# Moving first loads of a stage into the stage before it, and shortening the router's choose and place steps, in a two-layer GLA / RG-LRU / mixture-of-experts kernel

## The reference, cut to what matters

```python
for layer in range(DEPTH):                       # 2
    if layer % 2 == 0: x = x + gla_mixer(x, ...)
    else:              x = x + rglru_mixer(x, ...)   # y @ w_out inside
    x = x + hier_moe(x, ...)
return rmsnorm(x, final_norm)

def hier_moe(x, norm_w, w_group, w_expert, w_gate, w_up, w_down):
    h = rmsnorm(x, norm_w)
    g_sel = argmax(h @ w_group)                  # one group of 4
    logits = (h @ w_expert)[group g_sel]         # its 8 experts
    top_p, top_e = top_k(softmax(logits), 2)
    weights = p_g * top_p / sum(top_p)
    eid = g_sel * 8 + top_e
    # tokens are sorted by expert in blocks of 128 rows, and for each block
    y = (silu(xb @ w_gate[e]) * (xb @ w_up[e])) @ w_down[e]
    # summed per token with its two weights
```

## Time and profile before

| | us |
|---|---|
| median of three runs | 3212.1 |
| profiled execution, its own time | 3209.87 |
| its span | 3208.1 |
| route0 from / experts0 from | 878.7 / 1156.2 |
| lru from / route1 from | 1714.6 / 2280.2 |
| experts1 from / finish from | 2557.7 / 3096.5 |
| TensorE matmul busy | 2677.0 (83%) |
| VectorE busy | 1824.7 (57%) |
| ScalarE busy | 1626.1 (51%) |
| POOL busy | 588.3 (18%) |

### The profile page before, as it was taken

The page is one execution under the profiler, slowest core; times in us unless marked ns, Lnnn a source line. Parts: engine busy times, 40 slices in busy tenths (PEclk is TensorE's granted clock), DMA queues, the critical chain, the costliest instruction groups (busy, mean ns, idle before and its releaser), DMA issues. The chain is left out here.

```text
span 3208.1 us, 43209 instructions
## 1 busy us (share of the span) xinstructions
PE 2677.0 (83%) x12246; PEld 2126.9 (66%) x12246; DVE 1824.7 (57%) x3426; ACT 1626.1 (51%) x2253; POOL 588.3 (18%) x795
## 2 busy tenths in 40 slices
PE   4999969999789949999993999999599588999940
PEld 3777756777678837777772777777488466777730
DVE  3444443434356656657653688886466667656645
ACT  3445444444334436556653666666344266555533
POOL 0000000000001134545450000000011144545420
PEclk9999979999989979999996999999799789999975
DMA  3111121111154359888876445422444299977857
GB/s 102 44 46 52 35 83 39 32 47 52 59 199 144 124 197 325 282 281 293 299 245 223 163 167 172 167 99 86 159 138 144 86 342 342 314 253 262 288 224 274
DMA packets 358416, 552.11 MB, mean 172 GB/s; under 512 B 32128, under 2 KB 273936, under 8 KB 354192
## 3 DMA queue, kind: packets, MB, share of 16 engines
q1 hardware_dynamic: 323296, 436.20, 41.1%
q0 software_dynamic: 32688, 105.99, 8.8%
q10 hardware_dynamic: 2304, 8.39, 0.6%
HBM read 428.29 MB, written 122.22 MB: 172 GB/s over the span
## 5 line engine op out<-in xcount | busy, mean ns | idle before, releaser
L1384 DVE TENSOR_TENSOR experts_gu_lo<-experts_gu_raw,experts_gu_hi 128x1024 fp32r<-128x1024 f32 x256 | 296.5, 1220 | 83.8 <-ACT experts_gu_hi L1343 82.1
L118 PE MATMUL experts_ps<-experts_gu_hi,experts_hT_hi 128*128 128x512 f32 x760 | 318.3, 419 | 0.5 <-DVE experts_hT_lo L1395 0.5
L1266 POOL DMA_INDIRECT experts_rows<-h_rows,experts_source_now x194 | 261.9, 1350 | 273.8 <-PE experts_ps L1436 136.7
L119 PE MATMUL experts_ps<-experts_gu_lo,experts_hT_hi 128*128 128x512 f32 x760 | 301.7, 397 | 0.0
L120 PE MATMUL experts_ps<-experts_gu_hi,experts_hT_lo 128*128 128x512 f32 x760 | 299.9, 395 | 0.0
L1343 ACT ACTIVATE experts_gu_hi<-experts_gu_raw 128x1024 fp32r<-128x1024 f32 x256 | 249.9, 1055 | 74.2 <-DMA experts_gu_raw<-in_moe_w_up 74.2
L892 POOL MEMSET route_empty<- 128x512 int32 x2 | 1.1, 549 | 1445.0 <-POOLq L160 1445.0
L118 PE MATMUL route_ps<-route_w_hi,route_src_hi 128*128 128x512 f32 x512 | 213.1, 416 | 60.6 <-DVE route_w_lo L963 60.6
L1395 DVE TENSOR_TENSOR experts_hT_lo<-experts_ps,experts_hT_hi 128x512 fp32r<-128x512 f32 x194 | 132.9, 686 | 225.1 <-ACT experts_hT_hi L1322 223.8
L118 PE MATMUL gla_ps<-gla_wvg_hi,gla_hT_hi 128*128 128x512 f32 x512 | 212.1, 414 | 0.0
L1335 ACT ACTIVATE experts_y<-experts_ps,experts_by_block 128x1024 f32<-128x1024 f32 x99 | 110.6, 1117 | 199.0 <-DMA y_rows<-experts_y,experts_target_now 198.8
(11 more groups left out here) (300 smaller groups left out, 6528.1 us busy)
## 6 DMA issues: line engine op xcount, KB each, us to landing
experts_gu_raw<-in_moe_w_gate SPq DMA_DIRECT2D x64, 1024.0 KB
experts_gu_raw<-in_moe_w_up SPq DMA_DIRECT2D x64, 1024.0 KB
experts_wd_raw<-in_moe_w_down SPq DMA_DIRECT2D x64, 1024.0 KB, 5.7
gla_w_raw<-in_gla_w_in SPq DMA_DIRECT2D x18, 1024.0 KB, 6.6
route_src<-oT_rows SPq DMA_DIRECT2D x32, 512.0 KB, 4.3
x_rows<-route_x_new SPq DMA_DIRECT2D x32, 512.0 KB, 2.9
h_rows<-route_h SPq DMA_DIRECT2D x64, 256.0 KB, 2.3
lru_y_ab<-y_rows SPq DMA_DIRECT2D x16, 1024.0 KB, 7.6
```

The costliest lines, as they stand in the source:

```text
L118: nc.tensor.matmul(out, w_hi, x_hi, start=first, stop=False)
L119: nc.tensor.matmul(out, w_hi, x_lo, start=False, stop=False)
L1266: pool.indirect_dma_start(rows[:, b], None, h_halves[b], bass.IndirectOffsetOnAxis(source_now[b][:].bitcast(U32), 0))\
L1384: nc.vector.tensor_tensor(gu_lo[:, slot(e), of_part(c)], gu_raw[:, slot(e), of_part(c)], gu_hi[:, slot(e), of_part(c)].bitcast(F32), ALU.s ...
```

## The change

Four holders of on-chip memory are new. `Carry` is an arena of 32 KB a partition that lives from route0 to the end; in turn it holds a route's `w_raw`, the first slots `gu_raw` of the experts, one of lru's two `hT` buffers and the output projection of lru. `ExpertsAhead` holds the experts' raw weights from the route on, `LruEarly` the first x tiles, gain, parameters and raw weights of lru (wx and wg in the memory of `wd_raw`), `OutEarly` lru's output projection, `FinishEarly` six tiles of x and the gain.

- In tiles 14 and 15 of a route, SP first issues gate, up and down of experts 0 and 1 (`load_ahead`); before its tiles it waits for the last `w_lo`, since the arena is `w_raw` until then. `experts` itself loads only e+2 from then on.
- At the end of experts0, SP issues two tiles of x, the gain, wr, the eight parameter transfers and, when the last `wd_lo` is made, wx and wg. At the start of lru, only y is loaded.
- In lru's step 12, SP waits for TensorE's part of step 11 and issues the 4 MB of the output projection; route1 issues none.
- At the end of experts1, SP issues the gain and six tiles of x for `finish`, which is written out for all 16 tiles, without loop, with x in six buffers and squares written in bf16.
- `choose` takes 12 steps: instead of multiplying the logits by the group's one-hot row and adding up, it adds -3e38 to the other groups' and takes maximum and index over all 32. `place_tokens` takes 8: the totals start at 2048 times the expert's number, so that the rank holds the expert too, and the place is put together with shifts, an and and an or. Counting the blocks has one step more.

```diff
@@ project_and_route
-        w_raw = m.sb("w_raw", [P, PARTS, KD // PARTS, D])
+        w_raw = carry.raw[:].rearrange("p (a b c) -> p a b c", a=PARTS, c=D)
...
-                for a in range(PARTS if t == 0 else 0):
+                for a in range(PARTS if t == 0 and not out_early else 0):
                     sp.dma_start(w_raw[:, a], w_rows[a]).then_inc(w_in[a], DMA)
...
                 more = not (isinstance(t, int) and t >= NT - 2)
+                if not more:
+                    load_ahead(t - (NT - 2))
...
+            def load_ahead(e):
+                for into, w, landed in ((ahead.gu_raw[:, e, :, 0:FF], w_gate, ahead.gate_in),
+                                        (ahead.gu_raw[:, e, :, FF:], w_up, ahead.up_in),
+                                        (ahead.wd_raw[:, e], w_down, ahead.wd_in)):
+                    if e:
+                        sp.wait_ge(landed, DMA)
+                    sp.dma_start(into, w[e].rearrange("(k p) c -> p k c", p=P)).then_inc(landed, DMA)
+
+            sp.wait_ge(w_lo_done, nth(PARTS - 1))
             tiles(sp, body)
...
-            step.add(nc.vector.memset(total[:], 0.0))
+            step.add(nc.vector.tensor_scalar(total[:], k.expert_no[:], float(SLOTS * P), None, ALU.mult))
...
-                step.add(nc.vector.tensor_scalar(g_first[:], g_no[:], float(EPG), None, ALU.mult))
-                step(nc.vector.tensor_scalar(g_hot[:], k.expert_no[:, 0:GROUPS], g_no[:], None, ALU.is_equal))
+                step(nc.vector.tensor_scalar(not_mine[:], k.expert_no[:, 0:GROUPS], g_no[:], FAR,
+                                             ALU.not_equal, ALU.mult))
                 step(nc.vector.tensor_tensor(masked[:], experts[:],
-                                             g_hot[:].unsqueeze(2).to_broadcast([P, GROUPS, EPG]), ALU.mult))
-                step(nc.vector.tensor_reduce(mine[:], masked[:].rearrange("p g e -> p e g"), AX.X, ALU.add))
+                                             not_mine[:].unsqueeze(2).to_broadcast([P, GROUPS, EPG]), ALU.add))
...
-                step(nc.vector.max(top_e[:], mine[:]))
+                step(nc.vector.max(top_e[:], by_score))
...
-                step(nc.vector.tensor_scalar(e_no[:], e_no[:], g_first[:], None, ALU.add))
...
                 step(nc.vector.tensor_copy(rank_int[:], rank_now[:]))
-                step(nc.vector.tensor_scalar(blk_int[:], rank_int[:], 7, None, ALU.logical_shift_right))
-                step(nc.vector.tensor_copy(blk[:], blk_int[:]))
...
+                step(nc.vector.tensor_scalar(slot_int[:], rank_int[:], P - 1, ROW_SHIFT, ALU.bitwise_and,
+                                             ALU.logical_shift_left))
                 nc.vector.tensor_copy(entry[:, j, :, 0].unsqueeze(1), k.token[:, bass.ds(t, 1)])
-                nc.vector.tensor_copy(place_int[:, j], place[:]).then_inc(place_done, 1)
+                nc.vector.scalar_tensor_tensor(out=place_int[:, j], in0=rank_int[:], scalar=7, in1=slot_int[:],
+                                               op0=ALU.logical_shift_right, op1=ALU.bitwise_or)\
+                    .then_inc(place_done, 1)
@@ experts
-            load_gu(0)
-            sp.wait_ge(hT_ps_done, nth(1))
-            load_gu(1)
-            load_wd(0)
-            load_wd(1)
             for e in range(E - 2):
...
+            after_all(sp, lambda: sp.wait_ge(wd_lo_done, nth(E - 1)))
@@ lru
             for t in range(2):
-                load_x(t)
                 load_y(t)
-            sp.dma_start(gain[:], norm_w.partition_broadcast(P)).then_inc(gain_in, DMA)
-            load(wx, 0)
-            load(wg, 0)
             next_x(2)
-            load(wr, 0)
...
             for n in range(STEPS):
+                if n == STEPS - LRU_BLOCKS:
+                    after(sp, gb_ps_done, n - 1)
+                    for a, rows in enumerate(w_out.rearrange("(a b p) c -> a p b c", a=len(out_early.landed), p=P)):
+                        sp.dma_start(out_early.raw[:, a], rows).then_inc(out_early.landed[a], DMA)
@@ finish, SyncE (before: m.prime, the gain, then y and x of each tile in the loop)
+            for t in range(NT):
+                after(sp, x_done, t - DEPTH)
+                sp.dma_start(y_ab[:, t % DEPTH], y_tiles[t]).then_inc(y_in[t % DEPTH], DMA)
+                late = t + XD - DEPTH
+                if t >= DEPTH and late < NT:
+                    after(sp, h_done, late - XD)
+                    sp.dma_start(x[:, late % XD], x_dram[late * P:(late + 1) * P, :])\
+                        .then_inc(early.x_in[late % XD], DMA)
```

More of the change, by code:

```diff
@@ L820, in project_and_route @@
         HT_, LG, RK = 4, 6, 7
-        w_in = [m.plain(f"w_in{a}") for a in range(PARTS)]
+        w_in = out_early.landed if out_early else [m.plain(f"w_in{a}") for a in range(PARTS)]
+        m.held += out_early.held if out_early else []
         route_in, cleared, lists_clear = m.plain("route_in"), m.plain("cleared"), m.plain("lists_clear")
@@ L1074, in _ @@
             step(nc.vector.tensor_copy(nblk[:], nblk_int[:]))
+            step(nc.vector.scalar_tensor_tensor(out=nblk[:], in0=k.expert_no[:], scalar=-float(SLOTS), in1=nblk[:],
+                                                op0=ALU.mult, op1=ALU.add))
             step(nc.vector.tensor_scalar(nblk[:], nblk[:], 1.0, None, ALU.max))
@@ L1139, in project_and_route, with experts @@
         m.end()
-def experts(nc, k, stage, h_halves, lists_dram, w_gate, w_up, w_down, y_rows):
+def experts(nc, k, stage, h_halves, lists_dram, w_gate, w_up, w_down, y_rows, ahead, after_all):
     with ExitStack() as ctx:
@@ new lines, with __init__, load @@
+class FinishEarly:
+    TILES = 6
+    def __init__(self, nc, ctx):
+        m = Memory(nc, ctx, "finish_early")
+        self.x = m.sb("x", [P, self.TILES, D])
+        self.gain = m.sb("gain", [P, D])
+        self.gain_in = m.plain("gain_in")
+        self.x_in = [m.plain(f"x_in{j}") for j in range(self.TILES)]
+        self.held = m.held
+    def load(self, sp, x_dram, norm_w):
+        sp.dma_start(self.gain[:], norm_w.partition_broadcast(P)).then_inc(self.gain_in, DMA)
+        for t in range(self.TILES):
+            sp.dma_start(self.x[:, t], x_dram[t * P:(t + 1) * P, :]).then_inc(self.x_in[t], DMA)
@@ L1494, in lru @@
+def lru(nc, k, x_dram, y_rows, early, carry, out_early, w_out, w_in, conv_w, conv_b, w_r, b_r, w_i, b_i, lam, yT_dram):
     STEPS = NT // GT * LRU_BLOCKS
@@ L1496, in lru @@
         m = Memory(nc, ctx, "lru")
-        hT_hi = m.sb("hT_hi", [P, 2, KD, GROUP], F32R)
-        hT_lo = m.sb("hT_lo", [P, 2, KD, GROUP], F32R)
-        x = m.sb("x", [P, 2, D])
+        m.held += early.held
+        lent = carry.split[:].rearrange("p (a k c) -> p a k c", a=2, k=KD)
+        hT_hi = [lent[:, 0], m.sb("hT_hi", [P, KD, GROUP], F32R)[:]]
+        hT_lo = [lent[:, 1], m.sb("hT_lo", [P, KD, GROUP], F32R)[:]]
+        x = early.x
         h = m.sb("h", [P, D])
@@ L1502, in lru @@
         y_ab = m.sb("y_ab", [P, 2, 2, D])
-        gain = m.sb("gain", [P, D])
+        gain = early.gain
         ss, std, rstd = m.sb("ss", [P, 1]), m.sb("std", [P, 1]), m.sb("rstd", [P, 1])
@@ L1954, in _ @@
             for j in range(DEPTH):
[L1955 removed]
+                act.wait_ge(stored[j], NT // DEPTH * DMA)
         @block.vector
@@ new lines, in build @@
+        with ExitStack() as held:
+            ahead = ExpertsAhead(nc, held, "ahead0", carry)
+            lru_early = LruEarly(nc, held, ahead)
+            project_and_route(nc, k, "route0", oT, gla_w_out[0], x[0], x1, h_halves, moe_norm[0], moe_w_group[0],
+                              moe_w_expert[0], lists, carry, None, ahead, moe_w_gate[0], moe_w_up[0], moe_w_down[0])
+            experts(nc, k, "experts0", h_halves, lists, moe_w_gate[0], moe_w_up[0], moe_w_down[0], y_rows, ahead,
+                    lambda sp, wd_free: lru_early.load(sp, wd_free, x1, lru_norm[0], *lru_ws))
+            out_early = OutEarly(nc, ctx, "out_early", carry)
+            lru(nc, k, x1, y_rows, lru_early, carry, out_early, lru_w_out[0], *lru_ws, oT)
@@ new lines, in build @@
+        with ExitStack() as held:
+            ahead = ExpertsAhead(nc, held, "ahead1", carry)
+            project_and_route(nc, k, "route1", oT, lru_w_out[0], x1, x2, h_halves, moe_norm[1], moe_w_group[1],
+                              moe_w_expert[1], lists, carry, out_early, ahead, moe_w_gate[1], moe_w_up[1],
+                              moe_w_down[1])
+            early = FinishEarly(nc, held)
+            experts(nc, k, "experts1", h_halves, lists, moe_w_gate[1], moe_w_up[1], moe_w_down[1], y_rows, ahead,
+                    lambda sp, _: early.load(sp, x2, final_norm))
+            finish(nc, k, x2, y_rows, early, out[0])
```

203 lines of the change are left out of this document (115 added, 88 removed).

## The result

Four runs of the changed kernel gave a median of 3141.86 (3136.13 to 3144.5), four of the kernel before 3211.89: ratio 0.978, 95% interval 0.9761 to 0.98. That is 70.0 less; 63.1 was forecast, and 3149, with a range of 3130 to 3174. The profiled execution has a span of 3139.0, 69.1 less.

| stage | before | changed | difference | forecast |
|---|---|---|---|---|
| constants and gla (same code) | 878.7 | 872.6 | -6.2 | 0 |
| route0 | 278.5 | 262.7 | -15.9 | -13.1 |
| experts0 | 557.4 | 560.1 | +2.7 | -5 |
| lru | 565.6 | 552.5 | -13.1 | -11.5 |
| route1 | 278.5 | 259.5 | -19.1 | -15.9 |

The account below looks back on a forecast made before the run. TensorE was taken as busy nearly throughout, so savings lie in seams between stages and where TensorE is not last to wait; the terms sum to -63.1, 3146.8 profiled, 3149 on the runs' median, range 3130 to 3174.

Parts of the forecast that it names:

- Finish: Last stage: first add 3.3 earlier, seven table loads of 1.28 gone (9.0), one stumble of 0.3 gone; -12.6.
- Start of lru: First add waits only for y, -6.8; the fourth tile's wait for x goes, -4.7; together -11.5.
- Routes, inner tiles: Steady state: TensorE's waits for VectorE's choice and clock drops go, a tile takes 14.07; -8.2 in route0, -8.0 in route1.
- rival A: Routes: the clock drops stay although the waits go, +9, 3158; chance 15%.
- Tails: Ends of the routes: VectorE's shorter choose and place after the last projection save 4.9 in each route, -9.8.
- Start of route1: First split of lru's output projection no longer waits for its weights: -3.0, bounds 2.7 and 3.6.
- Start of the experts: ScalarE's first splits no longer wait for weights, on which two of TensorE's waits hang: -6 each, -12.
- Rival B: The experts' starts are held by the gathered rows, only -0.5 each: +11, 3160; chance 15%.
- rival C: The experts' starts gain all that ScalarE waited, 11.9 each: 3137; chance 10%.
- Early loads at the experts' ends: 4 and 3.5 MB more in windows with half the transfer time free: +2, from 0 to +10.
- Rival D: Early loads are not free at the stage ends or in lru: +10, 3159; chance 12%.
- Rival E: Experts' y stores and row gathers land later in every block; cancels the gain at 0.64 a block; chance 3%.

Follow-up runs that it names:

- tables: The changed kernel with an unused exponential between square and root of every finish tile, forcing two table loads per tile: 3189.1, run once; finish 139.9.
- w_out_late: The changed kernel with lru's output projection loaded by route1 at its start, as before, not in lru's step 12: 3148.4, run once; route1 261.7.
- u_ahead: The changed kernel with the weights of experts 0 and 1 loaded at the experts' start, as before: 3153.7, ratio to before 0.982.
- hoist_hold2: The changed kernel with block counts read early and expert 2's gate and up held until the first block is multiplied: 3147.0, run once; experts0 554.2, experts1 540.9.
- late_wx: The changed kernel with lru's wx and wg issued at lru's start instead of the end of experts0: 3139.5, ratio to before 0.978.
- hoist: The changed kernel with every engine reading the eight block-count words at the start of its experts program: 3148.7, ratio to before 0.9809.

## Why the prediction was right, and where it was off

- **Finish**, -12.6 forecast, -14.2 measured. First add -3.4 (-3.3 forecast), seven loads of 1.28 as said (`tables`). The rest, 1.9, I put down to the loop, which no run took apart; the sum had it only as one stumble of 0.3. A tile without loads is 5.47 on average instead of 5.56, and the first, with one load, 6.70 instead of 8.12.
- **Start of lru**: -7.0 and -4.8 at the fourth tile, against -6.8 and -4.7; right (the prediction's own terms give 6.9 for the first). The stage is 13.1 shorter; the 1.3 more than these two lie within its scatter.
- **Routes, inner tiles**: the mechanism right, waits and clock drops went together as the sum had it, and rival A is out; the size too small, -11.1 and -10.8 against -8.2 and -8.0. The step that failed is the tile of 14.07, got by taking the idle time from a pair of tiles. TensorE's idle time is counted from the modelled end of a matmul, while matmuls start every 0.23: from the last one's start to the logits' it was 1.19 with a wait and is 0.23 without (1064.12 to 1065.31 before, 1090.98 to 1091.21 now), so a wait of 0.80 cost 0.96. The logits' matmuls take 1.87 where they took 1.95 in both tiles of a pair without a drop, 0.08 less. A pair with a drop took 1.43 more than one without. So 6 x 0.96 + 12 x 0.08 + 3 x 1.43 = 11.0 of the 11.1.
- **Tails**: 4.9 and 4.8 against 4.9; right.
- **Start of route1**: 3.4 between the traces, 2.2 by `w_out_late`, against 3.0; right within the scatter of this start.
- **Start of the experts**, the step that failed in its place: 6 in each, and TensorE's waits taken to hang on ScalarE's late weights. Experts0 had 2.3 at the fourth y store, and by `u_ahead` 0.3 over the stage; experts1 9.0 and 11.4. I had read experts0's start and taken experts1's to be the same. The rows of experts0 could have said it: the first gate matmul had waited for hT_lo only 0.48, and POOL paused 4.99 with no releaser at all. What stands ahead of the first gate matmul is the gathered rows and TensorE's own down matmuls of the empty block; the third y store hangs on the reads and on the transfers behind them together (`hoist_hold2`). In experts1 it is the number of blocks an expert has that makes the weights late. Rival B holds for experts0, with the reads of the block counts as a cause that it did not name, and rival C nearly for experts1.
- **Early loads at the experts' ends**, +2 forecast. From the tenth last y store to the end the stages are 4.5 and 2.5 longer than before in the changed kernel's trace, 2.4 and 1.0 in the median of eleven, so 3.4 where 2 was forecast. In experts0 1.3 of it is wx and wg (`late_wx`); the rest is not taken apart. Rival D's +10 is out. Rival E is out too: from the fourth y store to the tenth last experts0 takes 427.8 (427.3 before) and experts1 400.5 (397.5), less than 0.1 a block, where it needed 0.64.
- **gla**, not in the sum: -6.2 for the same code. I take it for scatter, the trace of before being the slowest of 14 in gla; but there is only one trace of before. Without it the two traces differ by 62.9, the changed code's part, while the medians of all runs differ by 66 to 70.
- **The total**: that these 62.9 meet the 63.1 of the sum is luck. The two experts' stages gained 9.2 less than forecast (7.7 of it in experts0), and the routes, lru and finish some 9 more.

## What to carry to other kernels

A short chain on a helper engine that made TensorE wait 0.8 in every second tile cost more than twice its waits here (11.1 for 4.8), in the clock and in the matmul pipeline; get that engine under TensorE's tile time and stop there. Loads moved into the stage before are worth what the first instruction waited for them only if nothing else stands behind that wait: look at every engine's start for pauses without a releaser, and at each instance of a stage, since the data (here one block an expert or two) can change what bounds it. Move early what is needed early; weights used 22 us into lru held back a y store near the end of experts0 by some 4, though most of that was made up. And look at more than one trace before a few us at the end of a stage are given a cause.

## What the runs showed of the hardware that I had not expected

Eight reads of a word from on-chip memory into a register held an engine for 5.0 to 5.2 us together (POOL 5.24, ScalarE 5.02), some 0.65 each; no wait showed them, and the pause went when they were moved (`hoist`). A y store of 0.5 MB by index, issued 1 us behind 2 MB of weights of another queue, released POOL after 8.8 us in experts0 and 8.5 in experts1 (`hoist`), and after 3.7 in both without them (`hoist_hold2`). After single waits of TensorE of 0.8 the granted clock fell in three of six cases in route0 and stayed at 1.00 where the waits were gone.
